# The first stage of a two-block transformer kernel, rebuilt so that the modulation product and the token work share one pass over the first weights

## The chip, the cores and the metric

One core of a Trainium2 chip runs the whole program; nothing is shared with other cores. The metric is the device time of one execution in microseconds, lower is better. The kernel before was run three times for time and once more with the profiler.

## The reference, cut to what matters

Two transformer blocks work on 256 tokens of width 2048; the first also sees 256 context tokens as keys and values. What the change touches is the head of the first block:

```
mod_l = silu(c)     @ w_ada + b_ada      # w_ada is 2048 x 12288; 6 parts: sh_a, sc_a, gt_a, sh_f, sc_f, gt_f
mod_c = silu(c_ctx) @ w_ada + b_ada
h_l = rms_norm(x,   g_mix_norm) * (1 + sc_a)  + sh_a
h_c = rms_norm(ctx, g_mix_norm) * (1 + csc_a) + csh_a
qa, kva, kr, cb, cc, ch = split(h @ w_in)   # h_l for all columns, h_c for kva and kr only
```

Attention, a gated short convolution, the output product and a convolved FFN follow, then the whole second block. All is float32. Only the first two of the six parts are needed for the context (csh_a, csc_a), and for x they are needed first.

## The kernel before, in words

**Weights.** Every product streams its weights in chunks: one chunk is two rows of 128 by up to 512 columns (512 KB). SP issues the load of a chunk into one of 8 `raw` slots (L393). ACT copies it, rounded, into one of 4 `whi` slots (L581). DVE subtracts, which leaves the rest in `wlo` (L1039), and counts the raw slot free ("drained"). PE multiplies both parts and counts the split slot free ("chunk_used"). ACT and DVE run ahead of PE by up to 4 chunks; the function `ahead` on either engine writes one product's splits and places other work between them: `between` stands ahead of chunk 4, `later` at chunk 6, `side` ahead of the chunks it names.

**The first stage.** The first 8 groups of 8 chunks of w_ada give sh_a and sc_a for both token sets, with PE (L1888, L1889: the silu columns `cst` against the chunk, 512 columns of output, 4 matmuls a chunk). Each group's row of results is copied out by DVE (`mod_rows`, L1180), turned into columns by PE (L1875) and added to b_ada by DVE (`mod_cols`, into `mod_a`). Ahead of that stand, in order: all small vectors turned (L1851), all 64 tiles of x and ctx turned (L1859) and copied by DVE (L1165, to `xt` and `t16`), and the sums of squares (ACT L640 into `sq`, PE L1840, ACT root L647, DVE reciprocal L1122).

**The norms.** `norm_both` then makes the operand of x (`h1`) for all 16 tiles, and after it that of ctx (`hctx`) for all 16: per tile DVE multiplies by gain and root (L1139), ACT adds the shift and rounds (L655), DVE makes the rest (L1131). PE's first product (group KVG, 320 columns, both operands at once) waits for tile 2n+1 of `hctx` ahead of its chunk n, and so for the whole of `h1`.

**The other modulation parts.** The remaining 16 groups (128 chunks) of w_ada are for x alone. They are loaded between the weights of later products and summed by DVE (`sum_chunks`: L1066 or L1068, then L1071, two instructions a chunk into `acc`); a count per chunk of the product says how many. Such a chunk takes a raw slot and no split slot. PE folds a finished group with ones (`mod`, L1755) in the middle of the next product.

**After the norms** come, on every engine in the same written order: the KVG product, the q_a product, six convolution groups, with four small pairs of groups (QBG, KVB) and the attention steps (`att1`: scores L2019 and L2020, DVE maximum L1373, ACT exp L783, turns, values) woven in, then w_out (until about 620 us), and the FFN. The order is written by hand; each engine's queue is in order.

Of the kernel before, what the change touches and what calls it, by code (L numbers as in the profile page):

```python
# [8 lines left out]
P = 128  # L9
D = 2048  # L10
# [9 lines left out]
NACC = 2  # L20
# [152 lines left out]
UP_MODS = (8, 12, 16, 24)  # L173
PAIR_AFTER = {0: 0, 1: 1, 3: 2, 5: 3}
# [7 lines left out]
def program(nc, ins, consts, out, known, traced):  # L182
    with ExitStack() as ctx:
# [14 lines left out]
        s_x_in = sem("x_in")  # L198
        s_rope_in = sem("rope_in")
# [85 lines left out]
        conv_root = sb("conv_root", [P, 8, 8])  # L285
# [20 lines left out]
        sb("rest_of_t16", [P, 4 * T - 2 * T - P], scope=sc)  # L306
# [52 lines left out]

        def pair_parts(t, s, mixed=False):  # L360
# [11 lines left out]
        def cols(name, i, n):  # L372
# [4 lines left out]
             for n in ("w_ada", "w_in", "w_q_b", "w_kv_b", "w_out", "w_up", "w_down")}  # L377
        W.update({n: ins[n].rearrange("(k p) n -> p k n", p=P)
                  for n in ("w_in_2", "w_proj_a_2", "w_proj_b_2", "w_out_2", "w_up_2", "w_down_2")})
        flat = lambda t: t[:].rearrange("p k t -> p (k t)")  # L380
# [4 lines left out]
        def _(sp):  # L385
# [14 lines left out]
            def with_sum(name, c0, width=GW):  # L400

                for k in range(0, KT, KC):
                    load(W[name], k, KC, c0, width)
                    load_mod(1)
# [28 lines left out]
            for n, at in enumerate(CONV_COLS):  # L433
                with_sum("w_in", at)
# [136 lines left out]
        def _(act):  # L571
# [95 lines left out]
            row_src = {"c": ins["c"][0], "c_ctx": ins["c_ctx"]}  # L667
            for name in ("norm_mix_g_2", "norm_mlp_g_2", "norm_final_g_2", "g_final"):
                row_src[name] = ins[name]
            for name in ("b_ada", "g_mix_norm", "g_q_a", "g_kv_a", "g_mix_out", "conv_b", "g_ffn_norm", "ffn_conv_b"):  # L670
                row_src[name] = ins[name][0]
            for j in range(3):
                row_src[f"ffn_conv_w{j}"] = ins["ffn_conv_w"][0, j]
            row_src["conv_w"] = ins["conv_w"][0].rearrange("j n -> (j n)")
            for name, (g, r, n) in VEC_AT.items():
                act.dma_start(vrows[r:r + n, g, :], row_src[name].rearrange("(k p) -> k p", p=P)).then_inc(s_vec_in, 16)  # L676
            for tb in range(TB):
                act.dma_start(stage[:, 2 + tb, :], ins["ctx"][0, tb * P:(tb + 1) * P, :]).then_inc(s_x_in, 16)
            act.dma_start(bfb[:], ins["b_forget_2"].rearrange("(a n) -> a n", a=1).to_broadcast([P, HEADS]))\
                .then_inc(s_bias_in, 16)  # L680

            act.wait_ge(s_columns, L.of("columns", "vec"))
# [8 lines left out]
            def early():  # L691

                turn(4)
                squares(flat(xt))
                root(T, rstd[:, 0:T], D)
                squares(flat(t16))
                root(T, rstd[:, T:2 * T], D)

            ahead(STD, early)
            with L.loop(3):  # L700
                ahead(STD, turn)
                ahead(STD, turn)
            ahead(STD, turn)

            def norm_both():
                turn()
                act.wait_ge(s_columns, L.of("columns", "gain"))
                norm("h1", xt, h1, lambda k: mod_a[:, k, 0:1], True)
                norm("hctx", t16, hctx, lambda k: mod_a[:, k, 1:2], True)

            ahead(KVG, norm_both, None, 1)
# [97 lines left out]
            ahead(STD, lambda: turn(2), None, 1)  # L809
            ahead(QBG, lambda: conv_in(1), split=split_pair)  # L810
            ahead(KVB, turn)
            ahead(STD, lambda: turn(2), None, 1, side={6: att1})
            ahead(STD, lambda: conv_in(2), None, 1, side={1: att1, 4: att1, 6: att1})
            ahead(QBG, lambda: conv_in(3), split=split_pair, side={0: conv_sums(0), 1: att1})
            ahead(KVB, turn)
            ahead(STD, lambda: turn(2), None, 1, side={1: att1, 6: att1})
            ahead(STD, lambda: conv_in(4), None, 1, side={0: conv_normed(0, 0), 1: att1, 3: conv_normed(0, 1), 4: att1, 6: att1})
# [212 lines left out]
        def _(dve):  # L1030
# [119 lines left out]
            V.tensor_copy(vec[:, 0, :], half()[:, 0, 0:P]).then_inc(s_columns, 1)  # L1150
            L.mark("columns", "vec")
            n1, n3 = VEC_ROWS[1], VEC_ROWS[3]
            hv = half()[:, 0:2, :].rearrange("p b (g n) -> p b g n", n=P)
            V.tensor_copy(vec[:, 1:3, 0:n1], hv[:, 0, 1:3, 0:n1]).then_inc(s_columns, 1)
            L.mark("columns")
            V.tensor_copy(vec[:, 3:6, 0:n3], hv[:, 1, 0:3, 0:n3]).then_inc(s_half_read, 1)
            L.mark("half_read")
# [4 lines left out]
            for tb in range(4):  # L1162
                dve.wait_ge(s_turned, L.of("turned", tb))
# [1119 lines left out]
```

## Time and profile before

| | us |
|---|---|
| median of 3 runs | 2789.34 (2785.67 to 2792.21) |
| the profiled execution's own time | 2786.36 |
| its span, first to last instruction | 2784.6 |
| PE busy | 2654.4 (95%) |
| DVE busy | 1749.5 (63%) |
| ACT busy | 1218.9 (44%) |

A row of the timeline gives the start, the time, the engine (SPq and ACTq are the issue of a DMA by that engine's sequencer), the line, what is written and read, and in brackets how long the engine had been idle and who released it. The reported time is 1.8 us above the span.

### The profile page before, as it was taken

Reading aid. Unit: us, or ns where it says so; the run is one execution under the profiler, and the core shown is the slowest. Engines: PE = TensorE matmul, PEld = TensorE weight load, DVE = VectorE, ACT = ScalarE, POOL = GpSimd, SP = SyncE. Lnnn points to the kernel's source line nnn. Section 1 sums busy time; section 2 is a strip of 40 time slices with the busy share of each in tenths; the row PEclk is TensorE's granted clock in tenths of the full one; section 3 lists DMA queues with packets and bytes.
Section 4 is the critical chain, followed back from the end, with each engine's and each line's share of the span. In section 5 each row is a group of like instructions: output and inputs, shape, how many; then the busy total and the mean of one; then the engine's idle time right before and its main releaser. Section 6 shows DMA issues by size and latency. Waiting matters only on the chain.

```text
span 2784.6 us, 51586 instructions
## 1 busy us (share of the span) xinstructions
PE 2654.4 (95%) x21496; PEld 2569.1 (92%) x21496; DVE 1749.5 (63%) x2032; ACT 1218.9 (44%) x1464; POOL 96.8 (3%) x196
## 2 busy tenths in 40 slices
PE   4969998898999999999999999999999999999998
PEld 3659887698999999999999999999999999999998
DVE  2988866677888674665556555555555555555554
ACT  2743333334545453453544344444444444434433
POOL 0000032310000000000000010000000000000000
PEclk9989999899999999999999999999999999999999
DMA  4968865675777656565555455566556666666662
GB/s 157 381 205 266 270 194 173 204 264 186 237 261 244 192 188 184 173 202 189 188 171 165 137 163 168 179 196 196 190 175 189 196 190 195 193 194 194 191 210 100
DMA packets 289062, 553.54 MB, mean 199 GB/s; under 512 B 19386, under 2 KB 28712, under 8 KB 288232
## 3 DMA queue, kind: packets, MB, share of 16 engines
q1 hardware_dynamic: 287544, 548.28, 61.8%
q8 instruction: 141, 2.31, 0.3%
q10 hardware_dynamic: 1328, 2.55, 0.3%
q14 instruction: 49, 0.40, 0.0%
HBM read 548.53 MB, written 2.10 MB: 198 GB/s over the span
## 4 chain that ended last, share of the span: by engine, by line
PE 84%; DVE 9%; issue 3%; ACT 2%; DMA 1%; POOL 1%; ACTq 1%; DVEq 0%; POOLq 0%; SPq 0%
PE half L1784 25%; PE half L1786 25%; PE half L1785 25%; DVE wlo L1039 3%; DVE acc L1068 1%; PE half L1818 1%; PE half L1820 1%; PE half L1819 1%; PE half L2059 1%; DVE acc L1071 1%; ACT whi L581 1%; DMA raw<-in_w_ada 1%; PE half L1840 1%; ACTq L676 0%; PE half L2020 0%
## 5 line engine op out<-in xcount | busy, mean ns | idle before, releaser
L1039 DVE TENSOR_TENSOR wlo<-raw,whi 128x1024 fp32r<-128x1024 f32 (+1 forms) x909 | 1089.1, 1211 | 812.8 <-ACT whi L581 810.6
L581 ACT ACTIVATE whi<-raw 128x1024 fp32r<-128x1024 f32 (+1 forms) x909 | 942.3, 1049 | 1074.3 <-PE half L1786 954.5
L1784 PE MATMUL half<-hf,whi 128*128 128x256 f32 x2400 | 670.3, 279 | 8.5 <-issue 5.0
L1785 PE MATMUL half<-hf,whi 128*128 128x256 f32 x2400 | 668.7, 279 | 0.0
L1786 PE MATMUL half<-hf,wlo 128*128 128x256 f32 x2400 | 668.6, 279 | 0.0
L1784 PE MATMUL half<-hid,whi 128*128 128x256 f32 x1712 | 475.3, 278 | 0.0
L1786 PE MATMUL half<-hid,wlo 128*128 128x256 f32 x1712 | 474.6, 277 | 0.0
L1785 PE MATMUL half<-hid,whi 128*128 128x256 f32 x1712 | 474.6, 277 | 0.0
L1784 PEld LDWEIGHTS half<-hf,whi 128*128 128x128 f32 x2400 | 453.0, 189 | 10.5 <-issue 5.7
L1786 PEld LDWEIGHTS half<-hf,wlo 128*128 128x128 f32 x2400 | 454.7, 189 | 0.0
L1785 PEld LDWEIGHTS half<-hf,whi 128*128 128x128 f32 x2400 | 452.0, 188 | 0.0
L1784 PE MATMUL half<-h,whi 128*128 128x256 f32 x1520 | 430.9, 283 | 17.1 <-issue 15.9
L1786 PE MATMUL half<-h,wlo 128*128 128x256 f32 x1520 | 424.9, 280 | 0.0
L1785 PE MATMUL half<-h,whi 128*128 128x256 f32 x1520 | 424.9, 280 | 0.0
L1786 PEld LDWEIGHTS half<-hid,wlo 128*128 128x128 f32 x1712 | 322.7, 189 | 0.0
L1784 PEld LDWEIGHTS half<-hid,whi 128*128 128x128 f32 x1712 | 321.7, 188 | 0.1
L1785 PEld LDWEIGHTS half<-hid,whi 128*128 128x128 f32 x1712 | 321.6, 188 | 0.1
L1784 PEld LDWEIGHTS half<-h,whi 128*128 128x128 f32 x1520 | 288.7, 190 | 18.8 <-issue 16.7
L1785 PEld LDWEIGHTS half<-h,whi 128*128 128x128 f32 x1520 | 289.0, 190 | 0.6 <-issue 0.2
L1786 PEld LDWEIGHTS half<-h,wlo 128*128 128x128 f32 x1520 | 289.2, 190 | 0.0
L1071 DVE SCALAR_TENSOR_TENSOR acc<-raw,silu_sb,acc 128x512 f32<-128x512 f32 x128 | 96.2, 752 | 4.5
L1068 DVE SCALAR_TENSOR_TENSOR acc<-raw,silu_sb,acc 128x512 f32<-128x512 f32 x112 | 84.2, 752 | 11.7
(280 smaller groups left out, 3067.0 us busy)
## 6 DMA issues: line engine op xcount, KB each, us to landing
raw<-in_w_up SPq DMA_DIRECT2D x288, 512.0 KB, 4.2
raw<-in_w_in SPq DMA_DIRECT2D x216, 512.0 KB, 3.8
raw<-in_w_down SPq DMA_DIRECT2D x212, 512.0 KB, 4.5
raw<-in_w_ada SPq DMA_DIRECT2D x192, 512.0 KB, 5.4
raw<-in_w_out SPq DMA_DIRECT2D x64, 512.0 KB, 4.8
raw<-in_w_proj_a SPq DMA_DIRECT2D x16, 512.0 KB, 4.6
raw<-in_w_proj_b SPq DMA_DIRECT2D x16, 512.0 KB, 4.1
raw<-in_w_up SPq DMA_DIRECT2D x16, 384.0 KB, 3.3
```

Of the source, the lines that this page charges most:

```text
L581: A(whi[:, s, 0:elems], raw[:, c, 0:elems], ACT.Copy).then_inc(s_hi_ready, 1)
L1039: V.tensor_tensor(wlo[:, s, 0:elems], raw[:, c, 0:elems], whi[:, s, 0:elems].bitcast(F32), ALU.subtract).then_inc(s_drained, 1)
L1068: V.scalar_tensor_tensor(a, w[:, 0, :], s[:, 0:1], a, ALU.mult, ALU.add).then_inc(s_dve_step, 1)
L1071: V.scalar_tensor_tensor(a, w[:, 1, :], s[:, 1:2], a, ALU.mult, ALU.add).then_inc(s_drained, 1)
L1784: mm(o, hi, x[:, 0:T], start=(k == 0 and b % 2 == 0), stop=False, skip_group_check=True)
L1785: mm(o, hi, x[:, T:2 * T], start=False, stop=False, skip_group_check=True)
L1786: return mm(o, lo, x[:, 0:T], start=False, stop=(k == nk - 1), skip_group_check=True)
L1818: mm(o, xh, hi, start=(k == 0), stop=False)
L1819: mm(o, xh, lo, start=False, stop=False)
L1820: ins_ = mm(o, xl, hi, start=False, stop=(k == nk - 1))
L1840: ins_ = mm(half()[:, 0, 0:width], ones[:], sq[:, j % 2, b * width:(b + 1) * width], start=(c + b == 0), stop=(c == chunks - 1 and b == pe ...
L2059: ins_ = mm(sum_bank[:, i * T:(i + 1) * T], ones[:], sq[:, n % 2, b * T:(b + 1) * T], start=(first and i + b == 0), stop=(last and b == 3) ...
```

## The change

The stage keeps its arithmetic and is laid out anew:

- **Loads.** ACT issues only c, c_ctx, b_ada and the two halves of x. SP starts with w_ada at once; from the ninth chunk on it puts one other load behind each chunk: two of ctx, 15 small vectors, the forget bias.
- **Modulation rows.** PE waits for c, c_ctx and b_ada alone, turns them, and begins with chunk 0. The loop over groups is written out.
- **Token work.** It is cut in 19 "fills" of at most 4 turns each, which PE does behind chunk `FILL_AT[f]`, in one of four separate PSUM banks. ACT copies x tiles (ahead of chunks 14 to 21), squares each half of x and ctx whole with a running sum (ahead of 22, 25, 28, 31; 128x2048 from `stage`, which replaces the 64 matmuls of sums), takes one root of 4 columns (32). DVE inverts it (33). PE spreads the roots over rows. DVE copies those (37), and takes the ctx tiles with the root multiplied in (42 to 49), then the vectors (50, 51).
- **Norms.** Tile by tile for both operands. DVE makes x's product; ACT makes ctx's (scale and shift in one), then rounds x's and ctx's; DVE makes both rests: 3 instructions on each engine a tile. The splits of the KVG product's chunks 4 to 7 stand among them (ahead of each the engines stop behind tiles 8, 11, 14 on DVE, and 7, 10, 13 on ACT).
- **Sums moved.** The KVG product carries no w_ada chunks any more; its 8 are added to four convolution groups, whose last two product chunks carry two each. `acc` has three slots for two, and one fold (`mod`) moves from the q_a product to the last w_out group.
- `conv_root` moves into space that `t16` leaves.

```diff
-NACC = 2
+NACC = 3
+FILLS = [("x", tb, q) for tb in range(2) for q in range(4)] + ["roots"] + \
+    [("ctx", tb, q) for tb in range(2) for q in range(4)] + ["vec a", "vec b"]
+FILL_AT = list(range(10, 18)) + [33] + list(range(38, 46)) + [46, 47]
+X_SQUARES_AT = (22, 25, 28, 31)
+CONV_SUMS = [(1,) * GC] * 2 + [(1, 1, 1, 1, 1, 1, 2, 2)] * 4
...
-            for tb in range(TB):
-                sp.dma_start(stage[:, tb, :], ins["x"][0, tb * P:(tb + 1) * P, :]).then_inc(s_x_in, 16)
-            group("w_ada", 0)
-            group("w_ada", GW)
-            groups("w_ada", 6, 2 * GW)
-            with_sum("w_in", QR, KVR + ROPE)
-            with_sum("w_in", 0)
+            extra = extra_loads()
+            for g in range(8):
+                for k in range(0, KT, KC):
+                    load(W["w_ada"], k, KC, g * GW, GW)
+                    if g > 0:
+                        next(extra, None)
+            group("w_in", QR, KVR + ROPE)
+            with_sum("w_in", 0, (1,) * GC)
...
+            def x_squares(n):
+                A(flat(sq), stage[:, n, :], ACT.Square, accum_out=token_sums[:, n:n + 1]).then_inc(s_act_step, 1)
+            def x_tile(f):
+                A(xt[:, 4 * q:4 * q + 4, tb * P:(tb + 1) * P], side_banks[f % 4].rearrange("p (k t) -> p k t", t=P), ACT.Copy)\
+                    .then_inc(s_x_taken, 1)
+            def norm_both():
+                for k in range(KT):
+                    act.wait_ge(s_columns, L.of("columns", "gain"))
+                    a, b = 2 * k % 4, 2 * k % 4 + 1
+                    if k >= 2:
+                        act.wait_ge(s_act_lo, L.of("act_lo", ("hctx", k - 2)))
+                    A(tmp[:, b, :], t16[:, k, :], ACT.Identity, scale=gain[:, k, 1:2], bias=mod_a[:, k, 1:2]).then_inc(s_modded, 1)
+                    act.wait_ge(s_normed, L.of("normed", ("h1", k)))
+                    A(h1[:, k, 0:T], tmp[:, a, :], ACT.Identity, bias=mod_a[:, k, 0:1]).then_inc(s_rounded, 1)
+                    act.wait_ge(s_modded, L.of("modded", k))
+                    A(hctx[:, k, 0:T], tmp[:, b, :], ACT.Copy).then_inc(s_rounded, 1)
+                    if k in (7, 10, 13):
+                        yield
...
+                    ins_ = tt(t16[:, 4 * q:4 * q + 4, at], bank_.rearrange("p (k t) -> p k t", t=P), r, ALU.mult)
...
-                norm("h1", KT, xt, lambda k: gain[:, k, 0:1], h1, lambda k: mod_a[:, k, 0:1])
-                dve.wait_ge(s_act_lo, L.at("act_lo"))
-                norm("hctx", KT, t16, lambda k: gain[:, k, 1:2], hctx, lambda k: mod_a[:, k, 1:2], T)
-            ahead(KVG, norm_both, None, 1)
+                for k in range(KT):
+                    if k >= 2:
+                        dve.wait_ge(s_act_lo, L.of("act_lo", ("hctx", k - 2)))
+                    V.scalar_tensor_tensor(tmp[:, 2 * k % 4, :], xt[:, k, :], gain[:, k, 0:1], rstd[:, 0:T],
+                                           ALU.mult, ALU.mult).then_inc(s_normed, 1)
+                    if k > 0:
+                        lows(k - 1)
+                    if k in (8, 11, 14):
+                        yield
...
-            ahead(STD, lambda: first_values(1), mod, 1, side={5: rotate(1), 6: att1}, third=(1, lambda: keys(1)))
+            ahead(STD, lambda: first_values(1), mod, CONV_SUMS[2], side={5: rotate(1), 6: att1}, third=(1, lambda: keys(1)))
```

The instruction order moves at three places that matter below. On ACT at the head of the program, before: the loads it issues, then four splits, then the squares (the names: `vrows` the vectors, `stage` the raw tokens, `whi` a split).

```order
L678 DMA stage<-in_ctx 128x2048 x2
L679 DMA bfb<-in_b_forget 128x8
L684 ACT_TABLE_LOAD
L684 ACTIVATE silu_sb<-vec 128x32
L688 ACTIVATE cst<-silu_sb 128x2x16
L581 ACTIVATE whi<-raw 128x1024 x4
L640 ACTIVATE sq<-xt 128x1024 x4
L647 ACT_TABLE_LOAD
L647 ACTIVATE rstd<-half,eps 128x256
```

On the same engine in the changed kernel, from chunk 21 to the end of the w_ada groups:

```order
L731 ACTIVATE xt<-half 128x4x128
L612 ACTIVATE whi<-raw 128x1024
L718 ACTIVATE sq,stat<-stage 128x2048
L612 ACTIVATE whi<-raw 128x1024 x3
L718 ACTIVATE sq,stat<-stage 128x2048
L612 ACTIVATE whi<-raw 128x1024 x3
L718 ACTIVATE sq,stat<-stage 128x2048
L612 ACTIVATE whi<-raw 128x1024 x3
L718 ACTIVATE sq,stat<-stage 128x2048
L612 ACTIVATE whi<-raw 128x1024
L724 ACT_TABLE_LOAD
L724 ACTIVATE stat<-stat,eps 128x4
```

The four squares, one table load and the root now stand between splits of the same queue. On DVE, the part of the w_ada groups where ctx is taken (`t` is t16, `row` the modulation row), in the changed kernel:

```order
L1158 TENSOR_TENSOR t<-half,rstd 128x4x128
L1092 TENSOR_TENSOR wlo<-raw,whi 128x1024
L1243 COPY row<-half 4x512
L1158 TENSOR_TENSOR t<-half,rstd 128x4x128
L1092 TENSOR_TENSOR wlo<-raw,whi 128x1024
L1158 TENSOR_TENSOR t<-half,rstd 128x4x128
L1092 TENSOR_TENSOR wlo<-raw,whi 128x1024
L1158 TENSOR_TENSOR t<-half,rstd 128x4x128
L1158 TENSOR_TENSOR mod_a<-half,vec 128x8
```

Each of these eight splits has a take from PSUM ahead of it; before, the takes stood ahead of all w_ada splits. Further on DVE, the end of the group whose `between` is `first_values(1)`, before (from the maximum of the first attention step on):

```order
L1373 TENSOR_REDUCE stat<-half 128x1
L1105 TENSOR_TENSOR mod_f<-half,vec 128x4
L1039 TENSOR_TENSOR wlo<-raw,whi 128x1024
L1068 SCALAR_TENSOR_TENSOR acc<-raw,silu_sb,acc 128x512
L1071 SCALAR_TENSOR_TENSOR acc<-raw,silu_sb,acc 128x512
L1039 TENSOR_TENSOR wlo<-raw,whi 128x1024
```

and the same place in the changed kernel:

```order
L1456 TENSOR_REDUCE stat<-half 128x1
L1158 TENSOR_TENSOR mod_f<-half,vec 128x4
L1092 TENSOR_TENSOR wlo<-raw,whi 128x1024
L1121 SCALAR_TENSOR_TENSOR acc<-raw,silu_sb,acc 128x512
L1124 SCALAR_TENSOR_TENSOR acc<-raw,silu_sb,acc 128x512
L1121 SCALAR_TENSOR_TENSOR acc<-raw,silu_sb,acc 128x512
L1124 SCALAR_TENSOR_TENSOR acc<-raw,silu_sb,acc 128x512
L1092 TENSOR_TENSOR wlo<-raw,whi 128x1024
```

Two more sums stand behind each of that group's last two splits, ahead of the next split and the next maximum.

## Rows read from the trace of the kernel before

**Rows 1.** Windows: span, busy us (instructions) by engine, clock, DMA share, GB/s

```profile
0.00:26.00 26.00, 0.13 (x1) 0.16 (x2) 0.00 (x0) 1.28 (x1) 3.06 (x8) 1.00 0.91 322
26.00:64.00 38.00, 26.66 (x132) 23.52 (x133) 16.36 (x13) 14.24 (x16) 0.00 (x0) 0.96 0.19 67
64.00:146.00 82.00, 76.91 (x314) 52.39 (x313) 77.05 (x76) 63.97 (x62) 0.00 (x0) 0.98 0.98 355
146.00:173.00 27.00, 2.71 (x13) 2.17 (x11) 24.48 (x55) 11.93 (x23) 0.00 (x0) 0.56 0.52 186
173.00:207.00 34.00, 34.00 (x286) 34.00 (x287) 26.67 (x47) 12.16 (x20) 0.00 (x0) 0.95 0.57 186
...
308.00:349.00 41.00, 40.91 (x307) 36.11 (x306) 35.03 (x43) 12.71 (x16) 0.27 (x1) 0.98 0.85 279
349.00:393.00 44.00, 41.77 (x307) 37.22 (x308) 22.09 (x29) 15.95 (x36) 19.23 (x50) 0.96 0.52 162
```

**Rows 2.** Timeline of ACT and its DMA issues, 0 to 66 us

```profile
7.71 6.79 ACTq L676 DMA_DIRECT2D vrows<-in_ffn_conv_w  x3
14.52 5.82 ACTq L678 DMA_DIRECT2D stage<-in_ctx  x2
...
27.90 3.88 ACT L581 ACTIVATE whi<-raw 128x1024 fp32r<-128x1024 f32 x4
...
49.96 1.28 ACT L647 ACT_TABLE_LOAD   x1
...
54.64 2.00 ACT L640 ACTIVATE sq<-t 128x1024 f32<-128x1024 f32 x2 [1.82 <-DVE rstd L1122]
```

**Rows 3.** Timeline of DVE, 20 to 80 us

```profile
43.84 4.62 DVE L1039 TENSOR_TENSOR wlo<-raw,whi 128x1024 fp32r<-128x1024 f32 x4
...
76.17 0.67 DVE L1180 COPY row<-half 4x512 f32<-4x512 f32 x1
```

**Rows 4.** Timeline of ACT, a split in the middle of the w_ada groups

```profile
108.02 1.06 ACT L581 ACTIVATE whi<-raw 128x1024 fp32r<-128x1024 f32 x1 [0.29 <-DMA raw<-in_w_ada]
```

**Rows 5.** Timeline of DVE, from the last w_ada splits to the first ctx tiles

```profile
143.04 3.22 DVE L1039 TENSOR_TENSOR wlo<-raw,whi 128x1024 fp32r<-128x1024 f32 x3
...
148.27 0.75 DVE L1068 SCALAR_TENSOR_TENSOR acc<-raw,silu_sb,acc 128x512 f32<-128x512 f32 x1
...
152.10 0.82 DVE L1039 TENSOR_TENSOR wlo<-raw,whi 128x640 fp32r<-128x640 f32 x1
...
154.48 0.67 DVE L1180 COPY row<-half 4x512 f32<-4x512 f32 x1
157.11 0.17 DVE L1105 TENSOR_TENSOR mod_a<-half,vec 128x8 f32<-128x8 f32 x1 [1.96 <-PE half L1875]
...
157.61 1.27 DVE L1139 SCALAR_TENSOR_TENSOR tmp<-xt,gain,rstd 128x256 f32<-128x256 f32 x3
...
172.39 0.47 DVE L1131 SCALAR_TENSOR_TENSOR hctx<-tmp,mod_a,hctx 128x256 fp32r<-128x256 f32 x1
```

**Rows 6.** Timeline of PE, the first matmul of the KVG product

```profile
172.97 0.55 PE L1784 MATMUL half<-h,whi 128*128 128x256 f32 x1 [15.89 <-issue]
```

**Rows 7.** Timeline of ACT, the norms, and a split during the KVG product

```profile
158.19 1.31 ACT L655 ACTIVATE h<-tmp,mod_a 128x256 fp32r<-128x256 f32 x3 [6.58 <-DVE tmp L1139]
...
191.25 0.74 ACT L581 ACTIVATE whi<-raw 128x640 fp32r<-128x640 f32 x1 [3.34 <-PE half L1786]
```

**Rows 8.** Timeline of ACT: a copy from PSUM, the reading of a running sum

```profile
337.95 0.19 ACT L783 ACTIVATION_READ_ACCUMULATOR tmp<-half,stat 128x1 f32 x1
...
355.64 0.59 ACT L779 ACTIVATE sq<-half 128x512 f32<-128x512 f32 x1
```

**Rows 9.** Timeline of DVE, 200 to 400 us

```profile
207.51 0.69 DVE L1220 COPY kvraw<-half 128x512 f32<-128x512 f32 x1
...
387.29 0.96 DVE L1334 SCALAR_TENSOR_TENSOR qall<-half,rq 128x768 f32<-128x768 f32 x1 [5.24 <-PE half L1786]
```

**Rows 10.** The chain that ended last, 0 to 620 us: start, us, what

```profile
330.09 0.76 DVE acc L1068
```

More of the change, by code:

```diff
@@ L664, in norm @@
                 round_tiles(name, KT, lambda k: dst[:, k, 0:T], shift)
[L667 to L676, printed above, removed]
+            for name in ("c", "c_ctx", "b_ada"):
+                g, r, n = VEC_AT[name]
+                act.dma_start(vrows[r:r + n, g, :], row_src[name].rearrange("(k p) -> k p", p=P)).then_inc(s_cond_in, 16)
             for tb in range(TB):
[L678 to L682, printed above, removed]
+                act.dma_start(stage[:, tb, :], ins["x"][0, tb * P:(tb + 1) * P, :]).then_inc(s_x_in, 16)
+            act.wait_ge(s_half_read, L.of("half_read", "vec"))
             turn()
@@ L690, in _ @@
             L.mark("silu", "hi")
[L691 to L703, printed above, removed]
-            def norm_both():
[L706 to L709, printed above, removed]
@@ L711, in _, with x_roots @@
-            ahead(KVG, norm_both, None, 1)
+            def x_squares(n):
+                if n < TB:
+                    act.wait_ge(s_x_in, 32)
+                else:
+                    act.wait_ge(s_ctx_in, 32)
+                A(flat(sq), stage[:, n, :], ACT.Square, accum_out=token_sums[:, n:n + 1]).then_inc(s_act_step, 1)
+                L.mark("act_step")
+                act.wait_ge(s_act_step, L.at("act_step"))
+                yield
+            def x_roots():
+                A(token_roots1, token_sums, ACT.Sqrt, scale=1.0 / D, bias=eps[:]).then_inc(s_root, 1)
+                L.mark("root", "x")
+                yield
@@ L713, in kv_in @@
+            both_norms = norm_both()
+            ahead(KVG, lambda: (turn(), next(both_norms)), side={n: both_norms for n in (5, 6, 7)})
             def kv_in():
@@ L1190, in mod_cols @@
                 L.mark("half_read")
[L1192 to L1195 removed]
+            for g in range(8):
+                ahead(STD, mod_rows if g > 0 else None, (lambda: mod_cols(4 * g - 4)) if g > 0 else None,
+                      side={c: replies[GC * g + c] for c in range(GC) if GC * g + c in replies})
             def norm_both():
@@ L1452, in ffn_norm @@
             def ffn_norm():
+                mod()
                 into_ffn(3)
@@ L1856, in _ @@
-            for tb in range(4):
-                free()
-                for k in range(KT):
-                    ins_ = nc.tensor.transpose(half()[:, k // 4, (k % 4) * P:(k % 4 + 1) * P],
-                                               stage[:, tb, k * P:(k + 1) * P], ident[:])
-                ins_.then_inc(s_turned, 1)
-                L.mark("turned", tb)
-                turn()
-            pe.wait_ge(s_filled, L.of("filled", "ones"))
-            sums()
-            sums()
+            pe.wait_ge(s_filled, L.of("filled", "ones"))
@@ L1877, in turn_rows, with rows @@
                 L.mark("row_summed")
-            def rows(first=False):
+            def rows(g):
+                first = g == 0
                 if first:
@@ L1893, in rows @@
                         L.add("hi_ready")
+                        if GC * g + k // KC in fills:
+                            next(fills[GC * g + k // KC])
                 turn()
-            rows(True)
-            with L.loop(3):
-                rows()
-                rows()
-            rows()
+            for g in range(8):
+                rows(g)
             turn_rows(-1)
             def kv_sums():
-                n = L.n["squared"]
+                n = L.n.get("squared", 0)
                 pe.wait_ge(s_squared, L.of("squared", n))
```

199 lines of the change are left out of this document (141 added, 58 removed).

## The prediction

> **What bounds the kernel now.** Over the whole span PE is busy 95%, so I look first for stretches where it isn't. The busy time by stretch [rows 1] shows where: in the first 26 us PE does nothing and the DMA engines run at 322 GB/s; from 26 to 64 us the loads all but stop (67 GB/s), because the 8 raw slots are full and nobody splits; from 64 to 146 us the loads set the pace (355 GB/s over the stretch); from 146 to 173 us DVE alone is busy (24.5 of 27 us) and PE waits; from 173 us PE is full. So 173 us pass ahead of the first large product, and only the 82 us of the middle use the DMA engines fully. Then I look at how each of these ends.
>
> Start: ACT's sequencer is held by its own issues until 20.3 us [rows 2], the small vectors and ctx land behind them, and DVE makes its first w_ada rest at 43.8 us [rows 3].
>
> Middle: a split takes 1.06 us, and ACT idles 0.29 us before it for a load [rows 4]: a chunk comes every 1.35 us, which is 524 KB at 387 GB/s.
>
> End of the stage: DVE ends the last full w_ada rest at 145.4 us (the row at 143.04 ends at 146.26 and its third piece is a 640-wide one of 0.82 us), makes four KVG chunks with eight sums, copies the row at 154.48 us, waits 1.96 us for PE, and starts the norms at 157.61 us [rows 5]. The rests of the second ctx tile, which the first product chunk needs, start at 172.39 us, and PE starts at 172.97 us [rows 5, 6].
>
> The later convolution groups matter because work is added there. In 308 to 349 us DVE is busy 35.0 of 41 us [rows 1] and its sums stand in the chain that ended last [rows 10]; in 349 to 393 us it is busy 22 of 44.
>
> **The change part by part.** I count the times at which the stage's marks come.
>
> *Loads to chunk 22.* The first 26 us moved 8.4 MB [rows 1]; at 387 GB/s that is 21.6 us, so starting costs 4.4 us. By chunk 22 (the 23rd) the queues carry 23 x 0.524 MB, 4.2 MB of x and ctx, and 0.3 MB of small rows: 16.5 MB, 42.7 us, hence 47 us. ACT's own start isn't late: it issues five loads instead of 21, loads a table in 1.28 us, and each split before chunk 14 takes 0.97 us (3.88 for four [rows 2]) against 1.35 for a load. For chunks 14 to 21 ACT has a copy of 512 columns more, 0.59 us [rows 8]: 1.56 us a chunk, 0.2 us over the loads, together 1.5 us late. ACT is at chunk 22 at 48.5 us.
>
> *Chunks 22 to 31, on ACT.* Ten splits are 9.7 us. A square of 2048 columns is estimated as two of 1024, 2.0 us, with 0.19 us for the sum [rows 2, 8]: 8.8 us for four. The root needs another table, 1.28 us, and itself 0.3 (an estimate for four columns). Together 19.8 us where the loads need 13.5. With split 32 DVE can begin chunk 32 at 69.3 us. What hides such work in the slack of 0.3 us a chunk is soon used up, so I cost it in full.
>
> *Chunks 32 to 63, on DVE.* A rest takes 1.155 us (4.62 for four [rows 3]): 37.0 us. To that come four row copies of 0.67 and four column adds of 0.17 [rows 3, 5]: 3.4 us, and 11 takes of up to 512 columns from PSUM (the roots, 8 of ctx, two of vectors) of 0.69 each [rows 9]: 7.6 us. Sum 48.0, against 43.2 us for the loads. The last w_ada rest ends at 117.3 us instead of 145.4: **28.1 us earlier**. The bound below is that the squares and takes all hide in slack: then loads alone end the stage, 38.1 MB in 98.4 us, plus 4.4 to start and 2.3 for split and rest, 105.1 us.
>
> *From there to the norms.* Four KVG rests at 0.75 us each (0.82 less the overlap), without the eight sums, then 3.1 us from the row copy to the first norm as before (154.48 to 157.61): 6.1 us, where before it took 157.6 less 145.4, 12.2. **6.1 us earlier.**
>
> *From the norms to the product.* Before, 15.4 us. Now the first chunk needs tiles 0 and 1 of both operands. A stage of three instructions takes 1.2 us on DVE (three in 1.27 [rows 5]) and 1.3 on ACT (three in 1.31 [rows 7]); two tiles with the hand-over between the engines I put at 3.5 us. **11.9 us earlier.** Each further product chunk needs two tiles, 2.6 us on the slower engine, plus a split of 0.74; PE needs 0.74 + 3.34 = 4.08 us for one [rows 7]. So the rest of the norms hides behind PE. If that cover went (each tile in a full round of both engines, over 2 us), the product would become as slow as the norms, about 8 us lost at most.
>
> PE's first chunk begins cold in either kernel: the granted clock in 146 to 173 us is 0.56 [rows 1], and the pause after the last w_ada matmul stays over 6 us. No difference is counted.
>
> Together the KVG product starts 46.1 us earlier, at about 127 us.
>
> *The sums moved.* Removing them from the KVG product frees DVE where it had already been counted (above) or where PE is full. In four later groups each gets two more chunks: four instructions of 0.75 us [rows 5], 3.0 us a group, 12 us in all, and two loads of 1.35 us. Queued behind them on DVE are the next splits' rests and the next attention maximum, on which ACT's exp and then PE wait. The group with `first_values(1)` stands in the DVE-bound stretch: its 3 us I count in full, and the same for its like one round of the groups later. The other two end ahead of waits of DVE for PE such as 5.24 us [rows 9]; I count 0.75 each, for the maximum that comes later. **7.5 us given back**; the ends are 3 and 12.
>
> *At nothing.* The third `acc` slot, the moved fold (8 tiny matmuls and one add, once in either kernel), `conv_root`'s place. The fold in the last w_out group waits until DVE has read the group before it; cover is that group's first chunk, and without it 1 us is lost.
>
> **Sum:** 46.1 - 7.5 = 38.6 us. From the profiled execution's own 2786.4 that gives 2747.8; the median is 3.0 above that execution, and half of the three runs' spread is as large, so I forecast 2750.
>
> **A rule weighed against the trace.** The table load lasts 1.28 us in the row [rows 2]. The Trainium skill (ScalarE: Activation LUTs, "What ACT_TABLE_LOAD costs") gives 1283 ns for it, which the row bears out, and about 1380 ns of drain behind each switch, which no row here isolates. By the page the chain on ACT would be 1.4 us longer and the forecast 2751.
>
> **The rivals.**
>
> *Loads pace the whole stage.* For it: before, ACT had 0.29 us to spare for every chunk, and 8 slots hold 10.8 us of loads. Against it: the extra work comes in two lumps that sum to 6.3 + 4.8 us over the loads, and once DVE is late it has only 0.1 to 0.2 us a chunk to come back. It would give 12.2 us more, and with the low end of what is given back a gain of 50 to 56 us: 2733 to 2739.
>
> *The change gives back more than counted.* PE idles between attention steps later on, and those chains run through DVE and ACT (as before the row at 387 us [rows 9]); if all 12 us of sums lie on them, if the norms pace the product (8 us), or if the two lumps are met with more waiting between the three engines than the sums of single instructions say (5 us), the gain is 15 to 30 us: 2759 to 2774.
>
> *Slower: SP's queue.* The 15 small vectors, ctx and the bias now stand between w_ada loads in one in-order queue. The nearest row is ACT's: three small issues held its sequencer 6.79 us, and two of ctx 5.82 [rows 2]. If each of the 18 issues held SP that long (2.3 us for a small one, 2.9 for one of ctx), 42 us would be added, of which the slots hide some 10; the gain would still be about 7 us. It turns to a loss only from about 2.7 us apiece (48.6 over 18); at 3.5 us the time would be 2804. Against it: the 15 small issues ahead of those three were done by 7.71 us [rows 2], half a microsecond each, and the hold came when megabytes of other loads were queued; SP issues only when a slot is free.
>
> The Trainium skill (DMA: Bandwidth & Descriptors, "Rules for kernel authors") says that transfers under 64 KB are mostly overhead, and its table gives 0.68 us for 4 KB. By an estimate from the page, 16 small ones would cost 11 us of queue time, and the forecast would be some 10 us higher. No row here isolates one.
>
> *No change.* The stage could end where it did only if ACT's start were not freed; the small vectors that held it are gone from its queue, so I give this 1 in 100.
>
> **How the numbers follow.** Forecast (gain 30 to 50 us) 0.60, loads alone 0.17, more given back 0.18, no change 0.01, slower 0.04. A range of 2734 to 2764 holds the forecast, nearly all of the case of loads alone and a third of that of more given back, 0.82 in all; the forecast's own range is 2739 to 2759. What differs by under 0.2% (5.6 us) can't be told from no change here. Faster 0.95, same 0.01, slower 0.04.
>
> **What the changed profile would show.** The first w_ada split on ACT before 9 us; DMA at about 385 GB/s from there to 60 us; ACT without idle time from chunk 22 to 32; DVE without idle time from about 69 to 117 us and ACT released by PE there rather than by loads; the first KVG matmul at 127 us; matmuls of that product at 4.1 us a chunk; in the group with `first_values(1)` a DVE without idle time, and the end of w_out near 580 us instead of 620. I'm wrong if SP's issues show holds over 1 us between w_ada loads, if PE waits for `hctx` inside the KVG product, or if the 46 us seen at its start are down to under 30 at the end of w_out.

## The result and the profile after

| | before | after |
|---|---|---|
| median | 2790.78 us (4 runs, 2785.67 to 2793.1) | 2743.29 us (4 runs, 2738.22 to 2751.76) |
| ratio | | 0.9836, 95% interval 0.9812 to 0.986 |
| the profiled execution's own time | 2786.36 us | 2751.76 us |
| its span | 2784.6 us | 2749.9 us |

The kernel became 1.6% faster, and the forecast (2750, range 2734 to 2764) holds the median. The profiled execution of the changed kernel is the slowest of its four, so its span is 34.7 us shorter while the medians differ by 47.5.

The windows of the changed kernel, with the columns of [rows 1], cut where its own stages end:

```profile
0.00:26.00 26.00, 13.48 (x37) 8.51 (x37) 11.53 (x11) 11.77 (x13) 3.06 (x8) 1.00 0.94 354
26.00:48.00 22.00, 17.40 (x84) 13.73 (x84) 15.58 (x16) 16.58 (x22) 0.00 (x0) 0.84 1.04 375
48.00:69.00 21.00, 15.68 (x61) 10.68 (x62) 14.05 (x15) 19.33 (x21) 0.00 (x0) 0.92 0.98 344
69.00:117.00 48.00, 43.35 (x200) 32.53 (x199) 45.58 (x52) 32.91 (x33) 0.00 (x0) 0.93 0.93 316
117.00:130.00 13.00, 6.89 (x35) 6.08 (x34) 11.39 (x25) 9.39 (x21) 0.00 (x0) 0.79 0.72 238
130.00:164.00 34.00, 32.76 (x282) 32.56 (x281) 25.87 (x50) 19.58 (x40) 0.00 (x0) 0.98 0.48 142
```

The hole of 38 us at 67 GB/s is gone. The loads run at 344 to 375 GB/s up to 69 us; then DVE is busy 45.58 of 48 us and the loads fall to 316 GB/s: a load needs a raw slot, and DVE is what counts the slots free.

The timeline of ACT, from its first instruction to the root:

```profile
3.10 1.28 ACT L706 ACT_TABLE_LOAD   x1 [3.10 <-issue]
...
6.80 1.04 ACT L612 ACTIVATE whi<-raw 128x1024 fp32r<-128x1024 f32 x1
...
25.39 1.06 ACT L612 ACTIVATE whi<-raw 128x1024 fp32r<-128x1024 f32 x1 [2.78 <-DMA raw<-in_w_ada]
...
47.76 1.94 ACT L718 ACTIVATE sq<-stage 128x2048 f32<-128x2048 f32 x1
...
66.29 1.06 ACT L612 ACTIVATE whi<-raw 128x1024 fp32r<-128x1024 f32 x1
67.37 1.28 ACT L724 ACT_TABLE_LOAD   x1
68.67 0.30 ACT L724 ACTIVATE stat<-stat,eps 128x4 f32<-128x4 f32 x1
68.87 3.88 ACT L612 ACTIVATE whi<-raw 128x1024 fp32r<-128x1024 f32 x4
```

The first split ends at 7.84 us; ACT reaches chunk 22 and its first square at 47.76 us and is through the root at 68.97. Note the 2.78 us in front of the split at 25.39: a wait for a load, to which e2 comes back.

The timeline of DVE at the end of the stage, which answers to [rows 5], and the first matmul of the KVG product, which answers to [rows 6]:

```profile
115.59 5.46 DVE L1092 TENSOR_TENSOR wlo<-raw,whi 128x1024 fp32r<-128x1024 f32 x6
120.96 0.67 DVE L1243 COPY row<-half 4x512 f32<-4x512 f32 x1
122.78 0.17 DVE L1158 TENSOR_TENSOR mod_a<-half,vec 128x8 f32<-128x8 f32 x1 [1.14 <-PE half L1977]
...
123.28 0.88 DVE L1282 SCALAR_TENSOR_TENSOR tmp<-xt,gain,rstd 128x256 f32<-128x256 f32 x2
124.33 0.48 DVE L1272 SCALAR_TENSOR_TENSOR h<-tmp,mod_a,h 128x256 fp32r<-128x256 f32 x1 [0.18 <-ACT h L754]
124.74 0.42 DVE L1158 TENSOR_TENSOR hctx<-tmp,hctx 128x256 fp32r<-128x256 f32 x1
```

```profile
126.51 0.55 PE L1868 MATMUL half<-h,whi 128*128 128x256 f32 x1 [3.77 <-issue]
```

Of the six rests at 115.59 two are of w_ada and four of the KVG weights; the last one of w_ada ends near 117.9 us. Four weights later, with no sums between them, the row is copied, and 3.2 us after the first norm PE starts, where it took 15.4 us before.

What the program loses later shows in DVE's queue in the group with `first_values(1)`, the changed kernel's timeline first, then that of before at the same place:

```profile
276.25 0.68 DVE L1456 TENSOR_REDUCE stat<-half 128x1 f32<-128x512 f32 x1
...
281.70 0.75 DVE L1121 SCALAR_TENSOR_TENSOR acc<-raw,silu_sb,acc 128x512 f32<-128x512 f32 x1
282.49 0.75 DVE L1124 SCALAR_TENSOR_TENSOR acc<-raw,silu_sb,acc 128x512 f32<-128x512 f32 x1
...
285.66 0.75 DVE L1121 SCALAR_TENSOR_TENSOR acc<-raw,silu_sb,acc 128x512 f32<-128x512 f32 x1
286.44 0.75 DVE L1124 SCALAR_TENSOR_TENSOR acc<-raw,silu_sb,acc 128x512 f32<-128x512 f32 x1
...
289.89 0.68 DVE L1456 TENSOR_REDUCE stat<-half 128x1 f32<-128x512 f32 x1
```

```profile
326.28 0.68 DVE L1373 TENSOR_REDUCE stat<-half 128x1 f32<-128x512 f32 x1
...
336.64 0.68 DVE L1373 TENSOR_REDUCE stat<-half 128x1 f32<-128x512 f32 x1
```

Between two maxima lie 13.64 us where it was 10.36: 3.28 us for the four sums shown. DVE has one pause between them, 1.73 us behind the first maximum, and had it before (1.72 us), so the sums are paid in full and the lead of 50.0 us is 46.8 behind them.

The matmuls of w_out as a group (mean, median and longest ns, then first start to last start), changed kernel and before:

```profile
L1868 PE MATMUL half<-mix,whi x256: 276/281/561, 449.4 to 594.4; 128*128 128x256 f32 x128
```

```profile
L1784 PE MATMUL half<-mix,whi x256: 276/281/561, 489.0 to 632.3; 128*128 128x256 f32 x128
```

The lead is 46.5 us at the KVG product's start, 39.6 at w_out's first matmul and 37.9 at its last. From there the same work took 3.2 us longer in the changed kernel's profiled execution, which gives the 34.7 us between the spans.

### The profile page after: what moved, and what is told of

Read it like the earlier page. It is cut to its first block, busy times and chain, and to the rows that moved or that the text cites. A ratio compares the mean times of both kernels' runs of the same rounds, so it can differ in the third digit from the quotient of the medians.

```text
span 2749.9 us, 51222 instructions
## 1 busy us (share of the span) xinstructions
PE 2646.2 (96%) x21440; PEld 2561.8 (93%) x21440; DVE 1738.6 (63%) x2020; ACT 1224.0 (45%) x1487; POOL 102.9 (4%) x196
## 4 chain that ended last, share of the span: by engine, by line
PE 84%; DVE 9%; ACT 2%; issue 2%; DMA 1%; POOL 1%; SPq 0%; ACTq 0%; DVEq 0%; POOLq 0%
PE half L1868 25%; PE half L1869 25%; PE half L1870 25%; DVE wlo L1092 3%; DVE acc L1121 1%; DMA raw<-in_w_ada 1%; ACT whi L612 1%; PE half L1902 1%; PE half L1904 1%; PE half L1903 1%; DVE acc L1124 1%; PE half L2161 1%; PE half L1991 0%; PE half L2122 0%; PE half L2149 0%
```

## The experiments

Three marks tell more than the time: the first KVG matmul, the last start of a w_out matmul, and what lies between them. All are in us, from each kernel's profiled execution; medians and ratios are from the timed runs, against the kernel before on the same chip.

| | median | ratio, 95% | KVG starts | w_out ends | between |
|---|---|---|---|---|---|
| before | 2790.78 | | 172.97 | 632.3 | 459.3 |
| changed | 2743.29 | 0.9836 [0.9812, 0.986] | 126.51 | 594.4 | 467.9 |
| e0, changed | 2748.98 | 0.9852 [0.9835, 0.9869] | 127.10 | 592.1 | 465.0 |
| e9, changed | 2747.28 | 0.9859 [0.9834, 0.9883] | 126.07 | 591.1 | 465.0 |
| e1, sums back | 2744.25 | 0.9846 [0.9824, 0.9868] | 131.81 | 590.1 | 458.3 |
| e2, early squares | 2743.54 | 0.9832 [0.9818, 0.9845] | 122.98 | 590.5 | 467.5 |
| e3, norms in two passes | 2759.09 | 0.9889 [0.9875, 0.9903] | 136.23 | 599.8 | 463.6 |
| e4, light squares and takes | 2749.28 | 0.9848 [0.9825, 0.9872] | 119.25 | 586.6 | 467.4 |
| e5, vectors first | 2747.99 | 0.9849 [0.9824, 0.9874] | 131.86 | 598.9 | 467.0 |
| e6, e2 and ctx on ACT | 2746.23 | 0.9839 [0.9816, 0.9862] | 125.12 | 590.0 | 464.9 |
| e7, e6 and sums back | 2742.55 | 0.9831 [0.981, 0.9852] | 129.53 | 587.5 | 458.0 |
| e8, e2 and sums back | 2745.8 | 0.9855 [0.9834, 0.9876] | 130.74 | 591.0 | 460.3 |

**e0 and e9: the changed kernel again.**

> The changed kernel once more. Two marks of its first profile stand for theory and rival. Theory: the stage and the moved sums make all of the difference, so the first matmul of the KVG product starts at 126 to 127 us and the last matmul of w_out at 594 to 595 us (37 to 39 us earlier than before), in every execution, and what the total shows beyond or below 38 us comes from the unchanged 2150 us behind w_out and changes from execution to execution by up to 8 us either way; the ratio over five rounds is then 0.983 to 0.987. Rival: the executions of 2738 us are faster in the stage or in the convolution groups; then these two marks move by 5 us or more.

> The changed kernel again, on the same chip as its variant with both edits, so that the two times can be compared. By two earlier executions: first KVG matmul at 126.5 to 127.1 us, last w_out matmul at 592 to 594.4, 2743 to 2750 us.

Three medians of one kernel lie between 2743.3 and 2749.0, so a difference of 5 us between two columns of that table is nothing. The marks repeat better: KVG starts within 1.1 us, w_out ends within 3.3. (e0's theory had w_out end at 594 to 595 us in every execution; 592.1 and 591.1 miss that, by less than the rival's 5 us.) The windows from w_out's end to the end of the program show why. First e4, then e5, the same untouched work in both:

```profile
586.00:2747.50 2161.50, 2133.69 (x17838) 2108.93 (x17836) 1290.33 (x1425) 962.94 (x1097) 17.77 (x16) 0.99 0.59 188
```

```profile
598.00:2748.80 2150.80, 2121.68 (x17840) 2096.10 (x17839) 1290.03 (x1425) 963.04 (x1097) 18.89 (x16) 0.99 0.59 189
```

PE's busy time differs by 12.0 us over as many matmuls and the window by 10.7; over the windows cut like this in all twelve executions it spans 2150.8 to 2161.5. DVE's and ACT's busy times don't move. So an edit that is worth 12 us in the first 600 us can be missing from the span, as here, and I judge edits by the marks. The granted clock reads 0.99 in both; where the time goes is in the last section.

**e1: the sums back in the KVG product.**

```diff
-CONV_SUMS = [(1,) * GC] * 2 + [(1, 1, 1, 1, 1, 1, 2, 2)] * 4
+CONV_SUMS = [(1,) * GC] * 6
...
-            group("w_in", QR, KVR + ROPE)
+            with_sum("w_in", QR, (1,) * GC, KVR + ROPE)
```

> The changed kernel with the 8 chunks of sums back in the KVG product and one chunk per product chunk in all six convolution groups. Theory: the sums cost 11.3 us of DVE time between the last w_ada rest and the norms only for the four chunks that stand ahead of the norms (6.0 us later start of the KVG product: 132.5 us), and the 8.6 us that the convolution groups gave back come back; the last w_out matmul is then at 591 to 593 us, 2 to 3 us earlier than with the sums moved. Rival: the moved sums cost nothing in the convolution groups, the 8.6 us were lost to another wait there; then w_out ends 6 us later, at 600 us.

The product starts 5.3 us later and w_out still ends 2.4 us before the mean of the changed kernel's three (592.5). The timeline of DVE in e1 shows the sums between the last KVG rests, as before the change:

```profile
123.08 0.82 DVE L1092 TENSOR_TENSOR wlo<-raw,whi 128x640 fp32r<-128x640 f32 x1
124.00 0.75 DVE L1121 SCALAR_TENSOR_TENSOR acc<-raw,silu_sb,acc 128x512 f32<-128x512 f32 x1
124.78 0.75 DVE L1124 SCALAR_TENSOR_TENSOR acc<-raw,silu_sb,acc 128x512 f32<-128x512 f32 x1
125.45 0.67 DVE L1243 COPY row<-half 4x512 f32<-4x512 f32 x1
```

With the sums moved, the stretch between the marks lasts 463.6 to 467.9 us in eight executions; with them in place 458.0 to 460.3 in three. Moving them costs 7.1 us there (466.0, the mean of the changed kernel's three, less 458.9); the pairs that differ in nothing else say 7.7 (e1), 7.2 (e8 against e2) and 6.9 (e7 against e6). Where it goes, the attention maxima of e1 show, in its timeline of DVE:

```profile
283.72 0.68 DVE L1456 TENSOR_REDUCE stat<-half 128x1 f32<-128x512 f32 x1
294.09 0.68 DVE L1456 TENSOR_REDUCE stat<-half 128x1 f32<-128x512 f32 x1
...
367.80 0.68 DVE L1456 TENSOR_REDUCE stat<-half 128x1 f32<-128x512 f32 x1
381.42 0.69 DVE L1456 TENSOR_REDUCE stat<-half 128x1 f32<-128x512 f32 x1
```

The first two lie 10.37 us apart, as before the change, and not 13.64. The other two stand around the end of the group with `first_values(2)`: 13.62 us, where the changed kernel takes 17.34 (366.83 to 384.17). So these two groups pay 3.3 and 3.7 us. What the other two pay differs from one execution to the next: the one between them 0.3 to 3.7 us, the last from nothing to 0.5.

**e2: the squares where ACT waits for loads.** The splits at 25.39 us and the next but one waited 2.78 and 2.83 us: ctx's two halves of 1 MB lie between their loads, 2.7 us each at 387 GB/s. The squares of x fit there, and those of ctx move up.

```diff
-FILL_AT = list(range(10, 18)) + [33] + list(range(38, 46)) + [46, 47]
-X_SQUARES_AT = (22, 25, 28, 31)
+FILL_AT = list(range(10, 18)) + [28] + list(range(32, 40)) + [46, 47]
+X_SQUARES_AT = (9, 10, 22, 24)
```

> The changed kernel with the squares of x ahead of chunks 9 and 10 and those of ctx ahead of 22 and 24 (before: 22, 25, 28, 31), the roots spread behind chunk 28 (33) and the ctx tiles turned behind chunks 32 to 39 (38 to 45). Theory: the squares of x fall into two waits of ACT for loads of 2.8 us each (while ctx is loaded), which saves 4.2 us of ACT in the lump, and DVE's takes of ctx come while it waits for ACT; the last w_ada rest ends 6 to 9 us earlier (109 to 112 us for 117.9), the KVG product starts at 118 to 121 us, and that gain stays to the end: 6 to 9 us under the changed kernel. Rival: the stage is bound by the loads and the small row loads among them, and work placed earlier only moves waits; then the KVG product starts within 2 us of 126.5.

The timeline of ACT in e2 has the first square in the gap, and the split behind it waits no more for a load:

```profile
22.57 1.90 ACT L718 ACTIVATE sq<-stage 128x2048 f32<-128x2048 f32 x1
...
25.49 1.06 ACT L612 ACTIVATE whi<-raw 128x1024 fp32r<-128x1024 f32 x1 [0.93 <-ACT sq L718]
```

Of some 4 us of squares and more hidden, 3.6 us arrive at the KVG product, about half of the 6 to 9 that I expected, and 2.0 at w_out's end, which is within what repeats of one kernel differ by. DVE takes over as the bound earlier and is busy 54.35 of 56 us from 58 us on, so the lump on ACT was replaced by the work on DVE.

**e3: the norms in two passes, as before, all else as changed.** Cut to DVE's part:

```diff
-                    if k > 0:
-                        lows(k - 1)
+                    if k >= 2:
+                        low_x(k - 2)
+                for k in range(KT):
+                    dve.wait_ge(s_rounded, L.of("rounded", ("hctx", k)))
+                    tt(hctx[:, k, T:2 * T], tmp[:, k % 4, :], hctx[:, k, 0:T].bitcast(F32), ALU.subtract).then_inc(s_act_lo, 1)
```

> The changed kernel with the norms in two passes: all 16 tiles of x, then all 16 of ctx (multiplied by ACT as in the change). Theory: the first product chunk waits for the whole pass of x, 16 x 0.79 us on DVE, and two tiles of ctx: the KVG product starts 11 to 13 us later than in the changed kernel (138 to 140 us), and the total is 11 to 13 us longer. Rival: tile by tile the product is held back later by its own operands, so that half of the 12 us is lost again inside the product; then the last w_out matmul is only 5 to 8 us later than with both made tile by tile.

The timeline of DVE where the first norm stands, and of PE at its first matmul, in e3:

```profile
121.67 1.28 DVE L1281 SCALAR_TENSOR_TENSOR tmp<-xt,gain,rstd 128x256 f32<-128x256 f32 x3
```

```profile
136.23 0.55 PE L1870 MATMUL half<-h,whi 128*128 128x256 f32 x1 [15.09 <-issue]
```

From norm to product 14.6 us against 3.2: 11.4 us belong to the order of the norms alone. The product starts 9.7 us later (this execution reached its norms 1.6 us sooner) and w_out ends 7.3 us later than the mean of three. That is inside the rival's 5 to 8, but the 2.4 us that come back in between are less than the 2.9 by which the changed kernel's own executions differ there (465.0 to 467.9), so they don't decide for it. The time, 10 to 16 us above the changed kernel's three medians, is the only one of this study that is clearly apart.

**e4: less work in the two lumps.** ACT's squares read 128 of 2048 columns, DVE's takes of ctx 16 of 128 tokens; the kernel leaves the rest of that work out.

```diff
-                A(flat(sq), stage[:, n, :], ACT.Square, accum_out=token_sums[:, n:n + 1]).then_inc(s_act_step, 1)
+                A(sq[:, 0, 0:P], stage[:, n, 0:P], ACT.Square, accum_out=token_sums[:, n:n + 1]).then_inc(s_act_step, 1)
...
-                    ins_ = tt(t16[:, 4 * q:4 * q + 4, at], bank_.rearrange("p (k t) -> p k t", t=P), r, ALU.mult)
+                    ins_ = tt(t16[:, 4 * q:4 * q + 4, tb * P:tb * P + 16], bank_.rearrange("p (k t) -> p k t", t=P)[:, :, 0:16], r, ALU.mult)
```

> The changed kernel with its two lumps made light: each square covers 128 of 2048 columns and each take of ctx 16 of 128 tokens (the rest of t16 is cleared by GpSimd at the start), so 15/16 of the squares and 7/8 of the takes are left out. Theory: the lumps on ACT (7.2 us of squares) and DVE (some 4 us of takes) are what separates the stage from its loads; with them gone ACT waits for loads at almost every chunk from 22 on, the last w_ada rest ends at 108 to 111 us (117.9 in the changed kernel) and the KVG product starts at 117 to 119 us. Rival: the stage was held by SP's issues or by PE; then the KVG product starts at 124 us or later.

The last w_ada rest ends at 110.6 us, as expected, and the product starts at 119.25, 7.3 us earlier, for some 10 us of work taken off the two engines. The timeline of DVE in e4 shows who is left:

```profile
89.51 0.22 DVE L1160 TENSOR_TENSOR t<-half,rstd 128x64 f32<-128x64 f32 x1
89.76 1.22 DVE L1094 TENSOR_TENSOR wlo<-raw,whi 128x1024 fp32r<-128x1024 f32 x1
90.91 0.22 DVE L1160 TENSOR_TENSOR t<-half,rstd 128x64 f32<-128x64 f32 x1
```

DVE is still busy 44.53 of the 45 us from 69 to 114 us. Its last 31 rests with the small pieces among them take 41.7 us, 1.35 us a chunk, which is the loads' own 1.35: what DVE is behind by it can't make up. That is why the rival "loads pace the whole stage" stays out of reach even with light lumps. ACT waits for loads, as expected, only up to some 76 us; from there most of its waits end with PE.

**e5: the vectors ahead of x, on ACT's queue.**

```diff
-                for name, (g, r, n) in VEC_AT.items():
-                    if g > 0:
-                        sp.dma_start(vrows[r:r + n, g, :], row_src[name].rearrange("(k p) -> k p", p=P)).then_inc(s_vec_in, 16)
-                        yield
...
+            for name, (g, r, n) in VEC_AT.items():
+                if g > 0:
+                    act.dma_start(vrows[r:r + n, g, :], row_src[name].rearrange("(k p) -> k p", p=P)).then_inc(s_vec_in, 16)
```

> The changed kernel with the 15 small vectors issued by ACT ahead of x, as before, and out of SP's queue. Theory: ACT issues them in about half a microsecond each, so the silu and the first split come 7 to 8 us later (14 to 15 us), the 8 raw slots fill meanwhile, and since loads pace the stage until chunk 22 almost all of it is made good: the KVG product starts within 2 us of the changed kernel's 126.5 to 127.1. Rival (SP's queue): the small loads between w_ada loads held the stage back, and without them it is several us shorter: KVG product at 122 us or earlier.

Both sides missed. SP's issues of small loads in the changed kernel did hold longer than 1 us, seven of them, as its timeline shows for the longest:

```profile
21.91 3.20 SPq L447 DMA_DIRECT2D vrows<-in_conv_w  x1
```

Freed of them, the stage ends 5 us later. The timeline of ACT in e5 shows the price of the other place:

```profile
7.73 5.70 ACTq L699 DMA_DIRECT2D vrows<-in_ffn_conv_w  x3
13.46 3.61 ACTq L701 DMA_DIRECT2D stage<-in_x  x2
17.11 1.28 ACT L705 ACT_TABLE_LOAD   x1 [17.11 <-issue]
...
18.80 3.88 ACT L608 ACTIVATE whi<-raw 128x1024 fp32r<-128x1024 f32 x4
```

ACT's first split comes 12.0 us late, not the 7 to 8 expected, and 4.8 to 5.8 us of that remain at the product. That SP's holds cost less than ACT's I put down to the up to eight loads in flight ahead of them; no run tests it alone. The Trainium skill (DMA: Bandwidth & Descriptors, "Rules for kernel authors") calls transfers under 64 KB mostly overhead; the 10 us by which the prediction's estimate from that page would have delayed the product are not seen with the small loads on SP (126.1 to 127.1 us, forecast 127).

**e6: ctx taken by ACT.** On top of e2, PE multiplies ctx by a diagonal of roots, so that a copy by ACT does and DVE is spared 8 takes.

```diff
+                    V.tensor_scalar(root_diag[:, tb, :], ident[:], token_roots1[:, 2 + tb:3 + tb], None, ALU.mult).then_inc(s_normed, 1)
...
+                            ins_ = mm(bank_[:, i * P:(i + 1) * P], stage[:, 2 + tb, k * P:(k + 1) * P], root_diag[:, tb, :], start=True, stop=True)
```

> The kernel with early squares, and the root of ctx multiplied in by PE: its ctx tiles are turned against a diagonal of the roots (two DVE instructions of 128x128) instead of the identity, and ACT copies them where DVE multiplied. Theory: DVE bounds the early-squares kernel from chunk 26 on; without the eight takes of 0.71 us it has 49.5 us of work against 52 us of loads, so loads pace the stage to its end: last w_ada rest at 109 to 111 us (114.3 with early squares), KVG product at 118 to 119.5 us, 8 us ahead of the changed kernel, and the total 6 to 9 us under it. Rival: ACT, which takes the copies, or PE, whose turns become full products, holds the stage: KVG product at 122 us or later.

It went to the rival. Windows and then ACT's timeline in e6:

```profile
69.00:90.00 21.00, 20.87 (x127) 18.09 (x126) 15.65 (x16) 17.08 (x21) 0.00 (x0) 1.00 0.92 315
```

```profile
73.26 1.05 ACT L613 ACTIVATE whi<-raw 128x1024 fp32r<-128x1024 f32 x1
74.59 0.60 ACT L733 ACTIVATE t<-half 128x512 f32<-128x512 f32 x1 [0.28 <-PE half L1973]
```

PE is busy 20.87 of 21 us (17.82 in e2) and ACT waits for it in front of each copy. A chunk takes 1.82 us where e2's DVE needed 1.86, so nothing is won, and the product starts 2.1 us later than in e2. The engines lie so close together here that work taken off one makes the next one the bound.

**e7: e6 with the sums back**, and **e8: e2 with the sums back**; the edits are those above.

> The kernel with early squares and ctx on ACT, and the 8 chunks of sums back in the KVG product. Theory: the KVG product starts 5 us later than without the sums (124 us), and w_out ends 1 to 4 us earlier (583 to 586 us), since the sums cost more in the convolution groups than ahead of the norms. Rival: the two gains don't add, and w_out ends no earlier than in the kernel that has only the sums back (590 us).

> The two single edits that each moved a mark, together: the squares of x ahead of chunks 9 and 10 (and those of ctx at 22 and 24), and the sums back in the KVG product. If both add up as single runs showed them, the KVG product starts 3.5 to 4 us earlier for the first and 4.7 to 5.3 later for the second, near 128; the last w_out matmul stands at 586 to 588 us, against 590 to 594 of the changed kernel, and the time is 2 to 5 us below the changed kernel's of the same chip. Rival: the groups after the product have slack that takes up either edit alone, so that both give what one gives: 589 to 592 at w_out's end, and a time that can't be told from the changed kernel's.

e7 starts the product at 129.53, not near 124, and its mark at w_out, 587.5, lies between theory (583 to 586) and rival (590). It is the earliest of those that do all the work, but its 2742.55 can't be told from the changed kernel's 2743 to 2749. In e8 the early squares gain 1.1 us at the product over e1 (130.74 against 131.81), not 3.6, and w_out ends at 591.0: the rival's side. No version was found that beats the changed kernel by more than the measurement can tell.

## Why the prediction was right

The terms, as forecast and as the changed kernel's profiled execution shows them:

| term | forecast | measured |
|---|---|---|
| last w_ada rest | 28.1 earlier (117.3) | 27.5 (117.9) |
| from it to the first norm | 6.1 earlier | 6.8 (5.4 us instead of 12.2) |
| norm to product | 11.9 earlier | 12.1 (3.2 us instead of 15.4) |
| KVG product starts | 46.1 earlier (127) | 46.5 (126.51) |
| given back up to w_out's end | 7.5 | 8.6 here; 5.7 in e0, 5.7 in e9 |
| untouched rest of the program | 0 | 3.2 longer here; 1.9 and 2.8 in e0 and e9 |

*Chunks 0 to 31.* Chunk 22 came at 47.76 us (48.5), and DVE had split 32 at 69.9 (69.3). The squares took 1.89 to 1.94 us (2.0), the root 0.30 (0.3). The terms of this lump add up to 20.1 us, not the 19.8 I wrote; 21.2 were measured (47.76 to 68.97), since ACT idled a little among them, up to 1.01 us for a load, where I had said it wouldn't. The loads ran at 344 GB/s there, not 385.

*The table load.* It lasts 1.28 us at 67.37, the root follows at 68.67, and the split ahead of it ended at 67.35. The Trainium skill (ScalarE: Activation LUTs, "What ACT_TABLE_LOAD costs") gives a drain of about 1380 ns for a switch; 0.02 us are visible on either side, so the row's price was the right one here.

*Chunks 32 to 63.* DVE was the bound, with 45.58 of 48 us; e4 confirmed it by taking from DVE's takes and ACT's squares and finding DVE busy still, and e2 by freeing ACT and getting 3.6 us. As forecast, ACT was released by PE here: of its waits between 48 and 117 us, 14.7 us ended with PE and 1.5 with a load. The case "loads pace the whole stage" is refuted for this kernel: the loads ran at 316 GB/s from 69 us on, and even in e4 DVE had no time to spare.

*Norms.* Shown by e3: 11.4 us of the 12.1 come from making both operands tile by tile, and at w_out's end e3 is 7.3 us later (8.9 with its 1.6 us earlier start). PE never waits for `hctx` inside the product, the sign that would have spoken against this term. That PE begins alike in both kernels is not quite so: the granted clock over the product's first 15 us is 0.89 before and 0.83 in the changed kernel (118 and 111 matmuls), by those seven matmuls under 1 us.

*The sums.* The size is confirmed (7.1 us by e1, e7 and e8; forecast 7.5), and so are the two places that were counted in full, 3.3 us in the group with `first_values(1)` and 3.7 in the one with `first_values(2)` (forecast 3 each). What I hadn't put together is that the prediction's own second term, 6.1 us, is what moving them saves (5.3 by e1): the two cancel. This part of the change is worth nothing or costs up to 2 us. With the sums back, e1 still starts its product 41.2 us earlier than before, and these come from the woven stage and the norms.

*SP's queue.* I had called myself wrong if holds over 1 us appeared, and they did (up to 3.20 us), without the harm. The condition was badly chosen; e5 shows the alternative is dearer.

*The end of w_out.* "Near 580 us instead of 620" was a rough reading of the profile before; the rows give 632.3 and 591.1 to 594.4, a lead of 38 to 41 us.

*The median.* The ratios 0.9836, 0.9852 and 0.9859 mean 39 to 46 us, and the sum said 38.6. Since the repeats give 2747 to 2749, the first median was probably a low one by chance.

## What to carry to other kernels

A first stage should begin with whatever needs the fewest inputs, and the rest be woven in as single instructions; cost it by giving each engine its sum of instructions per chunk against the load's time, and let the largest set the pace, lumps included: an engine that is 0.1 us a chunk faster makes up 3 us in 32 chunks, not 10. Make a first product's operands in the order in which it eats them: that alone was 11 us at the product's start and 7 to 9 at w_out's end, and it cost no work. Count both ends of work that is moved from one busy stretch of an engine to another: here 5 us saved were 7 us spent.

## What the runs showed that I had not expected

The same 2150 us of untouched work differ by 10.7 us between executions, all of it in PE's busy time (2121.68 against 2133.69) at a granted clock that reads 0.99 both times. It isn't spread evenly. The windows of e4 and e5 over 60 us at the same distance from the end, 1560 us ahead of it:

```profile
1187.50:1247.50 60.00, 60.00 (x512) 60.00 (x511) 34.60 (x39) 25.06 (x26) 0.00 (x0) 1.00 0.55 193
```

```profile
1188.80:1248.80 60.00, 60.00 (x532) 60.00 (x531) 35.92 (x41) 27.24 (x28) 0.00 (x0) 1.00 0.63 217
```

PE is busy throughout at a clock of 1.00 and gets through 512 matmuls in e4 and 532 in e5; one lasts 281 and 276 ns on the mean. In this place eight of the twelve executions have 532 and four have 512 (the changed kernel's first, e2, e3, e4), with nothing between. 1920 us ahead of the end seven have 526 or 527, four 511 or 512, one 516. So whole stretches run at one of two paces, 3 to 4% apart, while the granted clock reads the same. What chooses the pace no run shows.

In the stretch between the KVG product and the first attention maximum the clock tells more. The windows of before and of the changed kernel there:

```profile
207.00:326.00 119.00, 113.93 (x905) 110.34 (x903) 104.01 (x135) 42.98 (x52) 0.00 (x0) 0.96 0.81 264
```

```profile
161.00:276.00 115.00, 109.05 (x902) 105.27 (x900) 104.30 (x134) 42.99 (x52) 0.00 (x0) 1.00 0.83 275
```

905 and 902 matmuls take 113.93 and 109.05 us at 0.96 and 1.00. From the KVG product's start to that maximum it is 153.3 us before, and 149.7, 152.3 and 149.5 in the changed kernel's three; so this is no gain of the change, and the 12.1 us that are lost between there and w_out's end in the changed kernel's first profile (50.0 down to 37.9) are partly bad luck: in that stretch PE is busy 281.31 us for 2030 matmuls, and in e0 275.53 us for 2028.

A small load can hold the sequencer that issues it for several times its usual half microsecond once large loads are queued: 3.20 us for one on SP at 21.91 us, 5.70 for three on ACT at 7.73.
